# Mixture-of-experts visits: picking and scattering token rows with one-hot matrices in fp32r passes over split halves instead of fp32 matmuls

## What is computed

```python
def moe_swiglu(xn, router, wg, wu, wd):
    xt = xn.reshape(B * T, D)
    logits = (xt @ router).astype(F32)
    topv, topi = lax.top_k(logits, TOP_K)
    gates = jax.nn.softmax(topv, axis=-1)
    combine = jnp.sum(jax.nn.one_hot(topi, N_EXPERTS) * gates[..., None], axis=1)
    y = jnp.zeros((B * T, D), F32)
    for e in range(N_EXPERTS):
        y = y + combine[:, e:e + 1] * swiglu(xt, wg[e], wu[e], wd[e])
```

## Time and profile before

| | |
|---|---|
| time, median of 3 runs | 2843.36 us (2839.74 to 2847.26) |
| the profiled execution's own time | 2846.78 us |
| its span in the trace | 2845.0 us |
| visits: first gate-up to end of the last scatter | 678.7 to 1743.6 us, eight of 132.2 us and the edges of the first and last |
| PE busy over the span | 2632.2 us (93%) |
| DVE, ACT busy | 1918.9 us (67%), 1398.1 us (49%) |
| DMA over the eight visits | 330 GB/s, 88.3% of 16 queues' time |

### The profile page before, as it was taken

The page is one execution under the profiler, slowest core; times in us unless marked ns, Lnnn a source line. Parts: engine busy times, 40 slices in busy tenths (PEclk is TensorE's granted clock), DMA queues, the critical chain, the costliest instruction groups (busy, mean ns, idle before and its releaser), DMA issues.

```text
span 2845.0 us, 46726 instructions
## 1 busy us (share of the span) xinstructions
PE 2632.2 (93%) x18471; PEld 2277.7 (80%) x18471; DVE 1918.9 (67%) x2883; ACT 1398.1 (49%) x2236; POOL 0.2 (0%) x4
## 2 busy tenths in 40 slices
PE   7887997997999999999999999999999988668898
PEld 6674997846989898989989899757999978445798
DVE  3765555746888888888888886857556554644554
ACT  1511433334777777777777785463444422143342
POOL 0000000000000000000000000000000000000000
PEclk9998998998999999999999999999999999889899
DMA  6535552575989898988888894204544532201451
GB/s 250 222 117 218 199 178 88 203 307 200 335 331 340 328 343 322 348 318 332 331 338 326 333 343 156 104 1 185 191 180 178 182 130 89 89 30 67 167 188 59
DMA packets 56568, 615.06 MB, mean 216 GB/s; under 512 B 6400, under 2 KB 6400, under 8 KB 6400
## 3 DMA queue, kind: packets, MB, share of 16 engines
q1 hardware_dynamic: 56160, 610.20, 57.2%
q10 hardware_dynamic: 288, 3.15, 0.3%
HBM read 612.28 MB, written 1.05 MB: 216 GB/s over the span
## 4 chain that ended last, share of the span: by engine, by line
PE 83%; DVE 10%; ACT 3%; issue 2%; DMA 2%; DVEq 0%; SPq 0%; ACTq 0%
PE psum L1603 7%; PE psum L1605 7%; PE psum L1604 7%; PE psum L314 6%; PE psum L316 6%; PE psum L315 6%; PE psum L504 5%; PE psum L1630 3%; PE psum L1632 3%; PE psum L1631 3%; PE psum L329 3%; PE psum L330 3%; PE psum L331 3%; PE psum L655 2%; PE psum L1262 1%
## 5 line engine op out<-in xcount | busy, mean ns | idle before, releaser
L398 DVE TENSOR_TENSOR r_high<-ring,r_high 128x1024 fp32r<-128x1024 f32 x936 | 1090.2, 1220 | 115.7 <-ACT r_high L360 114.4
L360 ACT ACTIVATE r_high<-ring 128x1024 fp32r<-128x1024 f32 x624 | 626.3, 1060 | 7.0 <-DMA ring<-stream_dram 7.0
L1603 PE MATMUL psum<-r_high 128*128 128x256 f32 x1792 | 513.7, 287 | 19.2 <-DVE r_high L1814 15.6
L1605 PE MATMUL psum<-r_high 128*128 128x256 f32 x1792 | 507.8, 283 | 0.0
L1604 PE MATMUL psum<-r_high 128*128 128x256 f32 x1792 | 507.4, 283 | 0.0
L314 PE MATMUL psum<-r_low,r_high 128*128 128x256 f32 x1408 | 402.4, 286 | 12.6 <-DVE r_high L474 12.6
L316 PE MATMUL psum<-r_low,r_high 128*128 128x256 f32 x1408 | 400.3, 284 | 0.0
L1603 PEld LDWEIGHTS psum<-r_high 128*128 128x128 f32 x1792 | 342.4, 191 | 47.2 <-issue 27.9
L1604 PEld LDWEIGHTS psum<-r_high 128*128 128x128 f32 x1792 | 342.8, 191 | 5.9 <-issue 1.7
L1605 PEld LDWEIGHTS psum<-r_high 128*128 128x128 f32 x1792 | 342.8, 191 | 0.0
L364 ACT ACTIVATE r_high<-ring 128x1024 fp32r<-128x1024 f32 x312 | 329.7, 1057 | 0.1
(11 more groups left out here) (470 smaller groups left out, 4185.7 us busy)
## 6 DMA issues: line engine op xcount, KB each, us to landing
ring<-stream_dram SPq DMA_DIRECT2D x384, 1536.0 KB, 8.2
arena<-bias_dram ACTq DMA_DIRECT2D x1, 2048.0 KB, 8.0
pack<-pack_dram SPq DMA_DIRECT2D x1, 1792.5 KB, 8.8
const<-const_dram SPq DMA_DIRECT2D x1, 1188.0 KB, 11.2
x<-x_dram SPq DMA_DIRECT2D x1, 1024.0 KB, 5.0
xc<-ctx_dram SPq DMA_DIRECT2D x1, 1024.0 KB, 25.5
arena<-band_dram ACTq DMA_DIRECT2D x1, 1024.0 KB, 4.9
out_dram<-x SPq DMA_DIRECT2D x1, 1024.0 KB, 3.9
```

The costliest lines, as they stand in the source:

```text
L360: act.activation(w_hi[:, i % 2, part * D:part * D + D], slot_of[r][:, part * D:part * D + D], ACT.Copy)\
L398: ins = dve.tensor_tensor(lo, slot_of[r][:, o:o + D], hi.bitcast(f32), SUB)
L1603: pe.matmul(dst, xe_hi[:, k, :], hi, start=(k == 0), stop=False)
L1605: ins = pe.matmul(dst, xe_lo[:, k, :], hi, start=False, stop=(k == KD - 1))
```

## The change

- The gather multiplies two halves of `xn` by `pick` in fp32r: a high part `row_parts` (made by ACT, two instructions of 128x1024) and a low part `xn_lo` (made by DVE, two of 128x1024). That is 4 fp32r matmuls for each chunk where there were 2 fp32 ones. `pick` is written as fp32r.
- `give` is gone. `giveT` is the transpose of `pick`, exactly one-hot, and the gate weight is put on as a scale for each place when the expert's output is evicted. For that, PE gathers the gate weights into a column with two fp32 matmuls of one column in block 2 of each visit, and DVE copies the column to `gate_s`.
- The output is evicted twice: ACT writes the scaled high part of both halves (two instructions of 128x512 where there was one), and DVE writes the scaled low part of both (two where there was one). The scatter is 4 fp32r matmuls on the high part and 4 on the low part, of 512 columns each; the high ones wait for ACT alone.
- `moe_more_visits_dve` is divided: the plan itself and the `vsel` table are made while DVE would wait for ACT inside `moe_xe_dve`; the `vpos` and `vwgt` tables stay behind the split of block 1.

```diff
         pick = parts(7168, NT * CAP, "p (j s) -> p j s", j=NT)
         giveT = parts(7680, NT * CAP, "p (j t) -> p j t", j=NT)
+        row_parts = parts(2048, 4096, "p (k t) -> p k t", k=KD)
+        xn_lo = parts(0, 2048, "p (j d) -> p j d", j=NT)
+        oute_hi = parts(7936, D, "p (h n) -> p h n", h=2)
+        oute_lo = [row_parts[:, 2 * h:2 * h + 2, 0:T] for h in range(2)]
...
+        def moe_pick_rows_pe(pe, dst, k):
+            for j in range(NT):
+                pe.matmul(dst, rows_hi(j, k), pick[:, j, :], start=(j == 0), stop=False)
+                ins = pe.matmul(dst, xn_lo[:, j, k * P:(k + 1) * P], pick[:, j, :], start=False, stop=(j == NT - 1))
+            return ins
...
             if i in (2, 3):
-                ins = pe.transpose(psum[:, 6 + b, 3 * P:4 * P], give[:, i - 2, :], ident)
+                ins = pe.transpose(psum[:, 6 + b, 3 * P:4 * P], pick[:, i - 2, :].bitcast(f32), ident)
+                if i == 2:
+                    for j in range(NT):
+                        ins = pe.matmul(psum[:, 6 + b, 2 * P:2 * P + 1], pick[:, j, :].bitcast(f32), gate_t[:, j:j + 1],
+                                        start=(j == 0), stop=(j == NT - 1))
             elif chunk is not None:
-                for j in range(NT):
-                    ins = pe.matmul(psum[:, 6 + b, 3 * P:4 * P], xn[:, j, chunk * P:(chunk + 1) * P], pick[:, j, :],
-                                    start=(j == 0), stop=(j == NT - 1))
+                ins = moe_pick_rows_pe(pe, psum[:, 6 + b, 3 * P:4 * P], chunk)
...
-                pe.wait_ge(sem("moe_out_act"), v + 1)
+                pe.wait_ge(sem("moe_out_act"), 2 * v + 2)
+                for j in range(NT):
+                    for hf in range(2):
+                        pe.matmul(psum[:, 2 * j + hf, :], giveT[:, j, :], oute_hi[:, hf, :], start=False, stop=False)
                 pe.wait_ge(sem("moe_out_dve"), v + 1)
                 for j in range(NT):
                     for hf in range(2):
-                        ins = pe.matmul(psum[:, 2 * j + hf, :], giveT[:, j, :], oute[:, hf * 512:(hf + 1) * 512],
-                                        start=False, stop=not more)
+                        ins = pe.matmul(psum[:, 2 * j + hf, :], giveT[:, j, :], oute_lo[hf], start=False,
+                                        stop=not more)
...
         def moe_act(act):
+            act.wait_ge(sem("norm_xn"), 4)
+            for j in range(NT):
+                act.activation(rows_hi(j), xn[:, j, :].rearrange("p (k e) -> p k e", k=KD), ACT.Copy)\
+                   .then_inc(sem("moe_rows_hi"), 1)
             split_act(act, experts, place(0, 0, 0, 0, 0), 0)
...
-                act.activation(oute[:, 0:512], psum[:, 4, :], ACT.Copy).then_inc(sem("moe_out_act"), 1)
+                for hf in range(2):
+                    act.activation(oute_hi[:, hf, :], psum[:, 4 + hf, :], ACT.Copy, scale=gate_s)\
+                       .then_inc(sem("moe_out_act"), 1)
...
-        def moe_give_dve(dve, v):
+        def moe_gate_dve(dve, v):
             for j in range(NT):
-                at = visit_col(v, j)
-                ins = dve.tensor_scalar(give[:, j, :], cst("iota"), vpos[:, at], vwgt[:, at], ALU.is_equal, MUL)
+                ins = dve.tensor_scalar(gate_t[:, j:j + 1], cst("ones")[:, 0:1], vwgt[:, visit_col(v, j)], None, MUL)
...
             ins.then_inc(sem("moe_xe_own"), 1)
+            moe_more_visits_dve(dve)
             dve.wait_ge(sem("moe_xe_own"), v + 1)
...
                 dve.tensor_copy(giveT[:, i - 2, :], psum[:, 6 + b, 3 * P:4 * P])
+            if i == 2:
+                dve.tensor_copy(gate_s, psum[:, 6 + b, 2 * P:2 * P + 1])
...
+        def moe_rows_lo_dve(dve, j):
+            dve.wait_ge(sem("moe_rows_hi"), j + 1)
+            hi = rows_hi(j).bitcast(f32)
+            step(dve, dve.tensor_tensor(xn_lo[:, j, :].rearrange("p (k e) -> p k e", k=KD),
+                                        xn[:, j, :].rearrange("p (k e) -> p k e", k=KD), hi, SUB), "dve_step")
...
             split_dve(dve, experts, place(0, 0, 0, 0, 0), 0)
+            moe_rows_lo_dve(dve, 0)
...
             S(dve.tensor_copy(vsel[:, 0:2 * N_EXP], sel.rearrange("p e j -> p (e j)")))
+            moe_rows_lo_dve(dve, 1)
...
             split_dve(dve, experts, place(0, 0, 0, 1, 0), 1)
-            moe_more_visits_dve(dve)
+            moe_more_values_dve(dve, ((vpos, pos), (vwgt, wgt)))
...
-                dve.wait_ge(sem("moe_dn"), v * NB_EXP + (NB_EXP + AHEAD))
-                dve.tensor_copy(oute[:, 512:1024], psum[:, 5, :]).then_inc(sem("moe_out_dve"), 1)
+                for hf in range(2):
+                    dve.wait_ge(sem("moe_out_act"), 2 * v + (hf + 1))
+                    ins = dve.scalar_tensor_tensor(oute_lo[hf], psum[:, 4 + hf, :].rearrange("p (k t) -> p k t", k=2), gate_s,
+                                                   oute_hi[:, hf, :].bitcast(f32).rearrange("p (k t) -> p k t", k=2), MUL, SUB)
+                ins.then_inc(sem("moe_out_dve"), 1)
```

More of the change, by code:

```diff
@@ L132, in program @@
         r_low = sb("r_low", LOW, f32r)
-        sb("arena_between", PARTS0 - LOW)
+        r_mid = sb("r_mid", PARTS0 - LOW, f32r)
         r_high = sb("r_high", 29696 - PARTS0, f32r)
@@ L155, in parts @@
         def parts(o, n, spec, **kw):
-            v = r_low[:, o:o + n] if o < PARTS0 else r_high[:, o - PARTS0:o - PARTS0 + n]
+            base, tile = (0, r_low) if o < LOW else (LOW, r_mid) if o < PARTS0 else (PARTS0, r_high)
+            v = tile[:, o - base:o - base + n]
             return v.rearrange(spec, **kw)
@@ L1546, in program @@
         xe = ar(6144, KD * CAP, "p (k s) -> p k s", k=KD)
[L1547 to L1550, removed]
+        pick = parts(7168, NT * CAP, "p (j s) -> p j s", j=NT)
+        giveT = parts(7680, NT * CAP, "p (j t) -> p j t", j=NT)
+        row_parts = parts(2048, 4096, "p (k t) -> p k t", k=KD)
+        xn_lo = parts(0, 2048, "p (j d) -> p j d", j=NT)
+        oute_hi = parts(7936, D, "p (h n) -> p h n", h=2)
+        oute_lo = [row_parts[:, 2 * h:2 * h + 2, 0:T] for h in range(2)]
+        gate_s, gate_t = sm("gate_s", 1), sm("gate_t", NT)
         before = ar(8960, P)
@@ L1582, in moe_count, with rows_hi @@
             return eng.value_load(plan_i[0:1, 0:1], min_val=N_EXP, max_val=MAX_VISITS)
+        def rows_hi(j, ks=slice(0, KD)):
+            return row_parts[:, ks, T + j * P:T + (j + 1) * P]
+        def moe_pick_rows_pe(pe, dst, k):
[3 more added lines that the diff above has]
+            return ins
         def moe_gather_pe(pe, v):
@@ L1588, in moe_gather_pe @@
                     k = 4 * half + c
-                    for j in range(NT):
-                        ins = pe.matmul(psum[:, 6 + half, c * CAP:(c + 1) * CAP], xn[:, j, k * P:(k + 1) * P],
-                                        pick[:, j, :], start=(j == 0), stop=(j == NT - 1))
+                    ins = moe_pick_rows_pe(pe, psum[:, 6 + half, c * CAP:(c + 1) * CAP], k)
                 ins.then_inc(sem("moe_gather"), 1)
@@ L1662, in moe_pe @@
                 moe_gate_up_pe(pe, place(0, 0, 0, i, 0), i, False)
-            pe.wait_ge(sem("moe_give"), 1)
+            pe.wait_ge(sem("moe_gate"), 1)
             def visit(v, more):
@@ L1863, in moe_weights_dve @@
             S(dve.tensor_copy(vwgt[:, 0:2 * N_EXP], wgt.rearrange("p e j -> p (e j)")))
-            moe_give_dve(dve, 0).then_inc(sem("moe_give"), 1)
+            moe_gate_dve(dve, 0).then_inc(sem("moe_gate"), 1)
         def moe_more_visits_dve(dve):
@@ L1878, in moe_more_visits_dve, with moe_more_values_dve, S @@
             S(dve.tensor_copy(plan_i[:, 1:12], plan_f[:, 1:12]), "moe_plan")
-            for dst, src in ((vsel, sel), (vpos, pos), (vwgt, wgt)):
+            moe_more_values_dve(dve, ((vsel, sel),))
+        def moe_more_values_dve(dve, pairs):
+            def S(ins, name="dve_step"):
+                step(dve, ins, name)
+            extra = MAX_VISITS - N_EXP
+            for dst, src in pairs:
                 for j in range(NT):
@@ L1884, in moe_more_visits_dve @@
                                     which_tmp.rearrange("p (j n) e -> p j n e", j=NT), AX.X, ADD))
-            S(dve.tensor_scalar(vpos[:, 2 * N_EXP:2 * MAX_VISITS], vpos[:, 2 * N_EXP:2 * MAX_VISITS], -float(CAP), None,
-                                ADD))
+            if dst is vwgt:
+                S(dve.tensor_scalar(vpos[:, 2 * N_EXP:2 * MAX_VISITS], vpos[:, 2 * N_EXP:2 * MAX_VISITS], -float(CAP),
+                                    None, ADD))
         def moe_dve(dve):
@@ L1914, in visit @@
                     if i == 3 and more:
-                        moe_give_dve(dve, v + 1)
+                        moe_gate_dve(dve, v + 1)
                         moe_pick_dve(dve, v + 1)
```

## The result

The changed kernel is slower by 0.2%: 2847.65 us against 2841.88 us, 20 runs of each, ratio 1.0020 with a 95% interval of 1.0011 to 1.0029. That is +5.8 us where the prediction has -4.4. One of the 20 executions of the changed kernel fell into a slow state, 4638 us at a granted clock of 0.71, and the ratio leaves it out. The profiled execution has a span of 2845.6 us.

The account below looks back on a forecast made before the run. PE's issue was taken to pace a visit, DVE a close second. Terms 3.6 - 2.5 - 2.1 - 1.0 - 2.4 = -4.4 us took the median from 2843.4 to 2839 us, range 2827 to 2869.

Parts of the forecast that it names:

- The step that failed: Visit edge, scatter to gate-up of block 2: DVE's queue lets 0.35 of 1.6 us arrive, -2.5 us over 7 edges.
- my terms for the visits: In the visits: gate column +3.6 us, edges -2.5, block 3 -2.1, last visit's wait -1.0.
- the chunks: Gather in the visits, 56 chunks: four fp32r matmuls cost 0.45 us, as the fp32 ones did; worth nothing either way.
- the price of the short pass: Gather's 128-column fp32r matmuls: 0.112 us each, bound by operand loads, with 0.065 and 0.224 as ends.
- The start: First visit: with less DVE table work ahead, PE restarts about 2.5 us earlier, -2.4 us.
- my bound of 1.8: First visit's restart: 1.8 us more gained if the shorter pause keeps the clock at 2.4 GHz.
- Neither 0.065 nor 0.224: Gather, us per short fp32r matmul: 0.065 if loads don't bind (chance 0.14), 0.224 if as dear as fp32 (0.22).
- The block-3 stall: PE's wait for give and pick at block 3: 0.67 us down to 0.35, -2.1 us over 7 visits.
- The gate column: Block 2 of each visit: four load-bound records cost PE 0.45 us, +3.6 us in all.
- a bound of +0.5: Last visit's end: scatter's saving goes into two evictions and the next split; nothing taken, bounds -1.6 and +0.5.
- the last line of the prediction: Says the forecast would be wrong above all by the gather's matmul distance, next by the clock at the start.
- the dear pass: Rival, gather: short fp32r matmuls cost 0.224 us like plain fp32, +28.7 us, 2868 in all; chance 0.22.

Follow-up runs that it names:

- E1: Changed kernel with 8 unread fp32 filler matmuls in PE's pause behind each visit's first transpose; 2837.9 us, ratio 0.9975 to the kernel before.
- E6: Changed kernel with give, giveT and the fp32 scatter as before, keeping the fp32r gather and divided plan; 2841.2 us, ratio 0.9984 to the kernel before.
- E5: Changed kernel with the old fp32 gather, keeping the changed scatter, gate column and divided plan; 2847.6 us, ratio 1.0005 to the kernel before.
- E7: Kernel before with three quarters of the scatter left out in every visit but the last; 2840.5 us, ratio 0.9985.
- E8: Changed kernel with 1 unread fp32 filler matmul in PE's pause behind each visit's first transpose; 2839.3 us, ratio 0.9980 to the kernel before.
- E2: Kernel before with half of the scatter left out in every visit but the last; 2833.3 us, ratio 0.9967.

## Why the prediction was wrong

**The step that failed** is this one: "Of the 1.6 us saved, 0.35 arrives: PE's wait grows from 0.87 to about 2.1." The wait was forecast to a tenth (1.99), and so was the restart: 9.89 us behind the eviction, against 10.12 before, a gain of 0.23. But I priced the wait as lost time alone. What it did to the clock of the work behind it is absent from the sum: 1.5 us in each of six visits and 1.0 in the last, 10 us in all by the visits of the changed kernel and E1. E1 puts a number on the rest: with the pause filled the middle visits are 0.6 us shorter than before and the last 0.9 (131.04 against 131.98), 4.5 us in all, where my terms for the visits give -2.0. About 2 us of the difference is the chunks, a term that I had put at nothing: by E6 the gather alone makes a visit 0.3 us shorter. With the clock's 1.5 us on top a middle visit is 0.9 longer. The rows were there to warn: I had noted a fall of the clock behind PE's pause at the start, and left it out of the visits because their windows showed 1.00 throughout. They did so with a pause of 0.87, not of 2. That the time lies inside my range of 2827 to 2869 is luck: the range was made wide for the price of the short pass, which held.

**The start** failed for a like reason. The divided plan gave 1.9 for the 2.4 forecast, and the full clock behind the shorter pause another 1.6, within my bound of 1.8 (E5); but the fp32r first gather brought the clock down by itself and cost 3.2. With it L1800's successor, which I had in its place within 0.2, starts 0.9 us later behind the gather's first matmul (7.06 against 6.15).

**Held:** the price of the short fp32r pass. I took 0.112 a matmul, 0.45 for four; measured 0.40: 0.11 for three, and 0.06 for the first. That 8 columns and 128 have the same distance fits my reading, that the load of the stationary operand binds and that the first load hides behind the longer matmul before it; no run changes the load alone. Neither 0.065 nor 0.224 came. The Trainium skill ("TensorE: Matmul & The Clock Gate", section "Back-to-back issue gap") has about 81 ns for a pair of load and matmul at 128 columns; the trace, with 0.11 us, does not agree with it. The scatter (four high and four low matmuls, 816.25 to 818.24 where gate-up of block 1 starts) took 1.99 for 1.84. The block-3 stall went from 0.67 to 0.39 for 0.35. The gate column costs PE its four records, and 0.26 of its 0.45 shows in the distance from the transpose to the next gate-up (2.02 against 1.76); the rest falls into a short wait that was there. The low-part evictions and the rows' high and low parts were covered, as forecast.

**The terms measured**, changed against before: six middle visits at +0.9, the last at +0.1, the start at -0.3 to the transpose in block 2, and +0.7 behind the last eviction, where the copy of x starts 4.35 us after it instead of 3.68. There I had taken nothing, with a bound of +0.5: a second eviction stands on ACT before the next stage's split. With 0.2 less in the rest of the first visit that is +5.7. Read at one go, from the gather's first matmul to the copy of x, it is 1077.1 us (671.56 to 1748.66) against 1071.5 (671.30 to 1742.80): +5.6, and the medians are 5.8 apart.

**The rivals.** None of mine named the clock, though the last line of the prediction had it second among what could go wrong, at the start alone. The one that I had put on the slower side, the dear pass, did not happen.

**Open:** what decides whether the clock falls behind a pause of 1.99 us; in E7 and E5 the same pause did both. One thing in the traces bears on it. In the changed kernel, in E5 and in E7, falls in neighbouring visits start 133.12 us apart, whether the visits last 133.1, 133.4 or 132.6. So in the changed kernel each fall comes 10.8 us behind the eviction, while in E5 it wanders between 9.8 and 10.9 and in E7 between 9.5 and 10.6. The moment of a fall is not set by the edge alone, and the edges of the changed kernel, which all meet it at the same place, are nearer to one observation than to seven. In E8 and E2 the visits last 131.6 and 131.1, so such a moment would lie elsewhere at each edge, and the clock held at all seven of each. That at this edge the clock fell behind the long pause alone is shown; that the long pause is enough is not.

## What to carry to other kernels

A pause has two prices: its own length, and the clock of the work behind it. Before shortening PE's work in front of a wait that won't move, look at what the pause will be, and either fill it or shorten the queue that sets it; here one DVE instruction moved by one block turned a loss of 0.2% into a gain of 0.3%. And when a window's clock goes from 1.00 to 0.99, cut the window until it reads 0.50.

## What the runs showed of the hardware

- At the edge of a visit the clock stayed at 2.4 GHz behind pauses of 0.87, 1.68 and 1.8 us, and behind one of 1.99 us it fell to 1.2 at seven of seven edges of the changed kernel, five of seven in E7 and six of seven in E5 (six of six, four of six and five of six in the middle visits). In the changed kernel it fell 0.9 us into the work behind the pause; in E5 and E7 the fall began between the moment of the restart and 1.4 us behind it. It came back about 3.4 us later, and each time it cost a middle visit 1.5 us.
- 32 fp32r matmuls of 128 columns in a row, 0.11 us apart, brought the clock to 1.2 GHz with no pause among them, some 2.5 us after the first, in all seven profiled executions that have them (six kernels). The 32 fp32 records at the same 0.11 distance, behind the same pause of 1.47 us, did so in none of five.
- An fp32r matmul of 128 columns costs 0.11 us where each has its own stationary operand, almost as much as one of 256 (0.12).
